# Last expert pair to its tokens through a matmul, the other expert rows loaded behind the last weights

## What is computed

```python
def hier_moe(u, w_group, b_group, w_router, b_router, w1, w3, w2):
    ...
    gate = p_grp * p_exp / jnp.sum(p_exp, axis=-1, keepdims=True)
    expert = g_sel * EXP_PER_GROUP + e_sel
    ...
    def expert_block(args):
        xe, e = args
        hid = jax.nn.silu(xe @ w1[e]) * (xe @ w3[e])
        return hid @ w2[e]

    yb = lax.map(expert_block, (xb, blk_e)).reshape(p_tot, d)
    out = jnp.zeros((n + 1, d), u.dtype).at[buf_tok].add(yb * buf_w[:, None].astype(yb.dtype))
    return out[:n]
...
    h = h + hier_moe(u, ...).reshape(b, t, d)
    return rmsnorm(h, norm_final_g)[:, N_META:]
```

## Time and profile before

| | us |
|---|---|
| median of 3 runs (2552.2 to 2559.76) | 2552.73 |
| the profiled execution, time | 2553.39 |
| its span | 2551.5 |
| PE busy / DVE busy / ACT busy / POOL busy | 2256.6 / 972.8 / 454.4 / 87.0 |

### The profile page before, as it was taken

How to read it: one execution, slowest core, us unless ns; L and a number is a source line. 1 busy time by engine, 2 the same in 40 slices (tenths; PEclk the granted TensorE clock), 3 DMA queues, 4 the chain that set the end, 5 groups by cost and what they waited for, 6 DMA issues and landing times.

```text
span 2551.5 us, 25973 instructions
## 1 busy us (share of the span) xinstructions
PE 2256.6 (88%) x9977; PEld 1536.2 (60%) x9977; DVE 972.8 (38%) x1962; ACT 454.4 (18%) x855; POOL 87.0 (3%) x118
## 2 busy tenths in 40 slices
PE   7999999988988999999899997788999688788882
PEld 5888887336753888887658774456785433223330
DVE  5454542232662554534420118866551310000003
ACT  2000000154361010001210024432013000000001
POOL 0000000000001000000110000000000000000000
PEclk9999999999999999999999998889999699988896
DMA  3232222211004232331132210000232599999994
GB/s 131 67 99 78 84 91 76 66 50 34 1 1 141 92 100 66 100 115 63 43 99 74 66 42 1 1 9 13 87 116 95 229 428 429 428 428 429 428 377 178
DMA packets 171350, 347.73 MB, mean 136 GB/s; under 512 B 17633, under 2 KB 146273, under 8 KB 154866
## 3 DMA queue, kind: packets, MB, share of 16 engines
q1 hardware_dynamic: 164960, 331.22, 35.0%
q0 software_dynamic: 5680, 12.99, 1.3%
q10 hardware_dynamic: 610, 2.17, 0.2%
HBM read 337.50 MB, written 16.98 MB: 139 GB/s over the span
## 4 chain that ended last, share of the span: by engine, by line
PE 67%; DMA 17%; DVE 7%; ACT 3%; DVEq 2%; issue 2%; SPq 0%; ACTq 0%; PEldq 0%; PEld 0%; POOLq 0%
PE PS L612 17%; DMA M<-w 11%; PE PS L643 10%; PE PS L69 7%; PE PS L3002 7%; PE PS L2367 5%; DMA M<-w_ffn_up 4%; PE PS L386 4%; PE PS L2549 2%; PE PS L924 2%; PE PS L1632 1%; PE PS L904 1%; DVE M L1958 1%; PE PS L988 1%; PE PS L1153 1%
## 5 line engine op out<-in xcount | busy, mean ns | idle before, releaser
L612 PE MATMUL PS<-M 128*128 128x256 f32 x2464 | 541.5, 382 | 16.4 <-DVE M L357 12.2
L612 PEld LDWEIGHTS PS<-M 128*128 128x128 f32 x2464 | 468.4, 191 | 90.3 <-issue 13.8
L3002 PE MATMUL PS<-M 128*64 128x512 f32 x1536 | 368.5, 639 | 86.0 <-DMA M<-w 81.6
L3002 PEld LDWEIGHTS PS<-M 128*64 128x64 f32 x1536 | 124.0, 147 | 319.0 <-issue 278.4
L643 PE MATMUL PS<-M 128*128 128x256 f32 x1232 | 268.9, 379 | 4.8 <-DVE M L731 2.5
L643 PEld LDWEIGHTS PS<-M 128*128 128x128 f32 x1232 | 233.4, 190 | 42.0 <-issue 10.8
L69 PE MATMUL PS<-M 128*128 128x264 f32 (+1 forms) x774 | 187.5, 403 | 16.5 <-DVE M L1701 5.4
L69 PEld LDWEIGHTS PS<-M 128*128 128x128 f32 x774 | 147.7, 193 | 55.4 <-issue 13.2
L3076 DVE TENSOR_TENSOR M<-M,PS 128x512 f32<-128x512 f32 x16 | 11.0, 687 | 420.9 <-PE PS L3002 420.9
L734 DVE TENSOR_TENSOR M<-M,PS 128x256 f32<-128x256 f32 x220 | 92.6, 421 | 200.8 <-PE PS L612 196.6
L2367 PE MATMUL PS<-M 128*128 128x264 f32 x616 | 142.9, 394 | 8.0 <-DVE M L2466 5.0
(11 more groups left out here) (381 smaller groups left out, 2279.0 us busy)
## 6 DMA issues: line engine op xcount, KB each, us to landing
M<-w SPq DMA_DIRECT2D x64, 2048.0 KB, 18.9
M<-w SPq DMA_DIRECT2D x64, 1024.0 KB, 21.4
M<-w_ffn_gate SPq DMA_DIRECT2D x22, 1024.0 KB, 5.4
M<-w_ffn_up SPq DMA_DIRECT2D x22, 1024.0 KB, 5.3
M<-w_ffn_down SPq DMA_DIRECT2D x16, 1024.0 KB, 5.1
M<-w_in SPq DMA_DIRECT2D x13, 1024.0 KB, 5.3
M<-w_in SPq DMA_DIRECT2D x25, 512.0 KB, 3.8
M<-w_ffn_down SPq DMA_DIRECT2D x8, 768.0 KB, 4.7
```

The costliest lines, as they stand in the source:

```text
L612: last = nc.tensor.matmul(PS[:, 3 * half + BANK[p], 0:HALF], lhs[:, a, :], rhs[:, a, :], start=p in FIRST and a == 0, stop=p in LAST and a ...
L3002: last = nc.tensor.matmul(PS[ROWS * k:ROWS * k + ROWS, bank, :], wide[:, a * P + ROWS * k:a * P + ROWS * k + ROWS], weights(k), start=star ...
```

## The change

1. `down_weights`: w2 comes in four transfers of 1 MB, in two halves of the contracted rows with a semaphore each, and `w2` has the halves outside and the banks inside. The same for all pairs.
2. `norm_final_g` is loaded at the start of the stage, ahead of w1 of the second pair, to where the gain of the earlier norm lay.
3. At the end of the routing DVE makes `C10["last"]`: for each choice of each token its gate if its pair is the last, else 0. Ahead of the last pair DVE makes ten tiles, for each of five token tiles and two choices, which have that gate in the token's slot of its row (L3123 of the kernel after), and TensorE multiplies each by the identity and sums over the choices, which gives `LAST_GATES`, slots by tokens.
4. The last pair is no more scattered. TensorE multiplies `LAST_GATES` by `YO`, two matmuls for each token tile (L3078), and DVE adds that from PSUM to `HN` (`last_pair`, L3157).
5. `rows_stored` is raised when the scatters of all other pairs have landed, and SP then loads `expert_rows` in four transfers of 1 MB and two small ones, behind the last weights in its program. Their buffers are elsewhere. The rows of the last pair in `expert_rows` are the zeros that lie there, so the weighted sum adds nothing for them.
6. The barrier behind the experts is gone, and semaphores of the routing are shared under new names.

```diff
-        C10 = {n: small(10) for n in ("rank", "pair", "half", "ob", "q", "in", "eid", "step")}
+        C10 = {n: small(10) for n in ("rank", "pair", "half", "ob", "q", "in", "eid", "step", "last")}
+        LAST_PAIR = small(1)
...
-        CG = [at(WORK0 + 18592 + 1024 * n, D) for n in range(10)]
-        GFIN = at(XN0, D)
+        CG = [at(base + 2 * D * n, 2, D) for base in (XN0, WORK0 + 8192) for n in range(2)]
+        CG4 = [at(HT0 + 3072, D), at(WORK0 + 12288, D)]
+        GFIN = GROW
+        LAST_SLOTS = [at(HT0 + 1024 + P * n, P) for n in range(8)] + [at(RG0 + 1024 + 640 + P * n, P) for n in range(2)]
+        LAST_GATES = at(RG0 + 1024, S2)
...
+            ts_(LAST_PAIR, PAIRS_F[:, 0:1], -1.0, None, ALU.add)
             then(ts_(EBI, EBF, float(EXPERTS - 1), None, ALU.min))
+            for j in range(2):
+                stt(C10["last"][:, 5 * j:5 * j + 5], C10["pair"][:, 5 * j:5 * j + 5], LAST_PAIR, C5[f"ga{j + 1}"],
+                    ALU.is_equal, ALU.mult)
+            dve.drain()
...
+            def down_weights(experts):
+                for part in range(2):
+                    for k in range(2):
+                        sp.dma_start(W2B[k][:, 2 * part:2 * part + 2, :],
+                                     expert("w2_2", experts[k], 4)[:, 2 * part:2 * part + 2, :]).then_inc(w2_in[part], 16)
...
+            sp.dma_start(GFIN, I["norm_final_g_2"].rearrange("(o n) -> o n", o=1).to_broadcast([P, D])).then_inc(gfin_in, 16)
             gate_weights(1, (1, BASE + 1))
...
-            for last in (2, 1):
-                pool.wait_ge(y_cp, pairs - last + 2)
-                scatter_rows(pool, pairs - last)
-            pool.wait_ge(y_st, pairs * 16)
+            rest = pool.value_load(PAIRS_I[0:1, 1:2], min_val=1, max_val=SPILL + 1)
+            pool.wait_ge(y_cp, rest + (BASE - 1))
+            scatter_rows(pool, rest + (BASE - 3))
+            pool.wait_ge(y_st, rest * 16 + 16 * (BASE - 2))
             pool.sem_inc(rows_stored, 1)
...
-                pe.wait_ge(w2_in, i * 32 + 32)
-                for half in range(2):
-                    for a in range(4):
+                for a in range(4):
+                    if a % 2 == 0:
+                        pe.wait_ge(w2_in[a // 2], i * 32 + 32)
+                    for half in range(2):
                         last = both(5 + half, HTT, lambda k: W2B[k][:, a, 512 * half:512 * half + 512], a,
                                     a == 0, a == 3)
...
+            pe.wait_ge(routing_given, 4)
+            for t, (lo, w) in enumerate(TOK_TILES):
+                dest = PS[:, 7, lo:lo + w] if w == P else PS[:, 4, 0:w]
+                for j in range(2):
+                    last = nc.tensor.matmul(dest, LAST_SLOTS[2 * t + j][0:w], ident[0:w, 0:w], start=j == 0, stop=j == 1)
+            last.then_inc(routing_made, 1)
             w1_w3(pe_last, 0, rest * 32 + (16 * AHEAD + 32))
+            pe.wait_ge(last_gates, 1)
             w2(pe_last)
+            pe.wait_ge(y_cp, pe_last + 2)
+            for t, (lo, w) in enumerate(TOK_TILES):
+                if t > 2:
+                    pe.wait_ge(hsum, t - 2)
+                for half in range(2):
+                    last = nc.tensor.matmul(PS[0:w, LAST_BANKS[t] + half, :], LAST_GATES[:, lo:lo + w],
+                                            YO[:, 512 * half:512 * half + 512], start=True, stop=True)
+                last.then_inc(last_added, 1)
...
+            for t, (lo, w) in enumerate(TOK_TILES):
+                for j in range(2):
+                    n = 5 * j + t
+                    ins = nc.vector.tensor_scalar(LAST_SLOTS[2 * t + j][0:w], C["iota"][0:w], C10["in"][0:w, n:n + 1],
+                                                  C10["last"][0:w, n:n + 1], ALU.is_equal, ALU.mult)
+            ins.then_inc(routing_given, 1)
+            dve.wait_ge(routing_made, 3)
+            nc.vector.tensor_copy(LAST_GATES[:, 0:S1], PS[:, 7, :])
+            nc.vector.tensor_copy(LAST_GATES[:, S1:S2], PS[:, 4, 0:META]).then_inc(last_gates, 1)
             hidden(dve_last)
             turned(dve_last)
...
+            def weighted(t):
+                w = TOK_TILES[t][1]
+                dve.wait_ge(comb_in[t], COMB_IN[t])
                 for j in range(2):
-                    ins = nc.vector.scalar_tensor_tensor(HN[0:w, t, :], CG[2 * t + j][0:w],
-                                                         C5[f"ga{j + 1}"][0:w, t:t + 1], HN[0:w, t, :], ALU.mult, ALU.add)
-                    if j:
-                        ins.then_inc(hsum, 1)
-                    else:
-                        dve.drain()
-                if t > 1:
-                    normed(t - 2)
+                    nc.vector.scalar_tensor_tensor(HN[0:w, t, :], rows_of(t, j)[0:w], C5[f"ga{j + 1}"][0:w, t:t + 1],
+                                                   HN[0:w, t, :], ALU.mult, ALU.add)
+                    dve.drain()
+
+            def last_pair(t):
+                w = TOK_TILES[t][1]
+                dve.wait_ge(last_added, t + 1)
+                row = HN[0:w, t, :].rearrange("p (c n) -> p c n", c=2)
+                nc.vector.tensor_tensor(row, row, PS[0:w, LAST_BANKS[t]:LAST_BANKS[t] + 2, :], ALU.add).then_inc(hsum, 1)
+
+            weighted(0)
+            weighted(1)
+            last_pair(0)
+            for t in range(2, 5):
+                weighted(t)
+                last_pair(t - 1)
+                normed(t - 2)
+            last_pair(4)
...
-            sp.wait_ge(stage_done, WORKERS * (PROJ2_STAGE + 6))
             sp.wait_ge(rows_stored, 1)
-            for t, (lo, w) in enumerate(TOK_TILES):
-                for j in range(2):
-                    sp.dma_start(CG[2 * t + j][0:w], y_dram[j * S2 + lo:j * S2 + lo + w, :]).then_inc(comb_in[t], 16)
-            sp.dma_start(GFIN, I["norm_final_g_2"].rearrange("(o n) -> o n", o=1).to_broadcast([P, D])).then_inc(gfin_in, 16)
+            by_choice = y_dram.rearrange("(j t) d -> t j d", j=2)
+            for t, (lo, w) in enumerate(TOK_TILES[0:4]):
+                sp.dma_start(CG[t], by_choice[lo:lo + w]).then_inc(comb_in[t], 16)
+            for j in range(2):
+                sp.dma_start(CG4[j][0:META], by_choice[S1:S2, j, :]).then_inc(comb_in[4], 16)
```

More of the change, by code:

```diff
@@ L2760, in route_act @@
         def route_act(act):
[L2761 to L2764, removed]
+            act.wait_ge(choice_in, 1)
+            nc.scalar.activation(GE, GE, ACT.Exp).then_inc(choice_out, 1)
+            act.wait_ge(choice_in, 2)
+            nc.scalar.activation(C5["ex"], C5["ex"], ACT.Exp).then_inc(choice_out, 1)
         def route_pe(pe):
-            pe.wait_ge(e_onehot, 1)
+            pe.wait_ge(routing_given, 1)
             columns = ES.rearrange("p t e -> p (t e)")
@@ L2778, in route_pe @@
                                             start=j == t == 0, stop=j == 1 and t == 4)
-            last.then_inc(buf_ready, 1)
+            last.then_inc(routing_made, 1)
         def route_dve(dve):
@@ L2818, in route_dve @@
             dve.drain()
-            tt(ES[:, 0:5, :], E12[:, 0], E12[:, 1], ALU.add).then_inc(e_onehot, 1)
+            tt(ES[:, 0:5, :], E12[:, 0], E12[:, 1], ALU.add).then_inc(routing_given, 1)
             def per_expert(name, values):
@@ L2919, in others @@
                 sp.wait_ge(y_done, i)
-                for k in range(2):
-                    sp.dma_start(W2B[k], expert("w2_2", experts[k], 4)).then_inc(w2_in, 16)
+                down_weights(experts)
             def pair(i, c):
@@ L2931, in experts_sp @@
             up_weights((0, BASE))
-            for k in range(2):
-                sp.dma_start(W2B[k], expert("w2_2", BASE * k, 4)).then_inc(w2_in, 16)
+            down_weights((0, BASE))
             sp.wait_ge(g_in, 16)
+            sp.dma_start(GFIN, I["norm_final_g_2"].rearrange("(o n) -> o n", o=1).to_broadcast([P, D])).then_inc(gfin_in, 16)
             gate_weights(1, (1, BASE + 1))
@@ L3125, in program @@
         OUT_DMAS = 5
+        COMB_IN = (16, 16, 16, 16, 32)
         def moe_sp(sp):
@@ L3139, in moe_sp @@
                 if out is not None:
-                    sp.dma_start(out[0, lo + first - META:lo + w - META, :], CG[2 * t][first:w]).then_inc(out_done, 16)
+                    rows = CG4[0] if t == 4 else CG[t][:, 0, :]
+                    sp.dma_start(out[0, lo + first - META:lo + w - META, :], rows[first:w]).then_inc(out_done, 16)
         def moe_pool(pool):
             first_rows_pool(pool); stage(pool, "pool")
-            experts_pool(pool); stage(pool, "pool")
+            experts_pool(pool)
             if dbg is not None: stage(pool, "pool")
@@ L3148, in moe_pe @@
             route_pe(pe); stage(pe, "pe")
-            experts_pe(pe); stage(pe, "pe")
+            experts_pe(pe)
             if dbg is not None: stage(pe, "pe")
@@ L3153, in moe_act @@
             route_act(act); stage(act, "act")
-            experts_act(act); stage(act, "act")
+            experts_act(act)
             final_act(act)
@@ L3159, in moe_dve @@
```

(2 more changed lines are left out.)

38 lines of the change are left out of this document (20 added, 18 removed).

## The result

The kernel after takes 2536.86 us (2532.16 to 2540.77), the kernel before beside it on the same chip 2552.73 (2550.76 to 2559.76). The ratio is 0.9927, 95% interval 0.9909 to 0.9946. The forecast was 2532.0 with 2526 to 2541: the time lies in the range, 4.9 us above the forecast and at the upper edge of its own range of 2527 to 2537; a second measurement of the same kernel (e10) got 2539.2. One run of the kernel after (3038.73 us, counted in its median alone) and one of e5 (3040.85 us), at mean granted clocks of 0.735 and 0.734, stand apart from all others and are in no range and no ratio here. The profiled execution took 2536.86, its span is 2535.0 us (before 2551.5).

The account below looks back on a forecast made before the run. The weight stream was taken to bound the expert stage, with a serial tail behind it. Terms -5.6 (last w2, start included), -18.7 (to first add), +2.7 (DVE), +0.3 (reload) took 2553.4 to 2532 us, range 2526 to 2541.

Parts of the forecast that it names:

- Bulk of the stage: nothing: Expert stage: splitting w2 into 1 MB transfers costs and gains nothing, as the stream stays at 428 GB/s.
- Start of the stage: +1.0: Stage start: extra DVE operations and the early norm_final_g shift the weight stream by 0 to 2.6 us, taken as 1.0.
- The slots-by-tokens matrix: Ahead of the last pair: DVE's ten tiles take 3.3 us, covered; TensorE's identity products add 2.5 us from 2474.1.
- w2 of pair 13 ends near 2450.3, 4.5 us earlier: Pair 13: TensorE starts w2 on its first half, ending 4.5 us earlier and filling the 2451 to 2457 us hole.
- the last w2: -5.6 us: Last pair: the last down-projection ends at 2503.0 for 2508.6, with the 1.0 us of the start included.
- The second then, since its weights are there by 2499.0 at the latest: Last w2: its second half runs directly behind the first, which ends at 2498.0, without waiting for weights.
- An idle time of 2.35 us or less did not bring it down: Last w2: idle time this short leaves the granted clock full, so 32 records take 7.3 us for 9.46.
- To the first add: From the last w2's end to DVE's first waiting add: 3.0 us in place of 21.7, a gain of 18.7.
- DVE behind it: DVE's work from that first add to its end: 21.5 us for 18.85 before, a cost of 2.7.
- Reload: +0.3: Expert-row loads: late landing of tile 0's rows delays DVE's combining by up to 1.8 us, taken as 0.3.
- (C): Rival, 10%: w2's halves don't land apart, w2 ends as before plus 1.0, clock low; +6.6 us, 2538.7.
- (B): Rival, 8%: row loads disturb the last weights' landing or start only after it; about 2541 us.

Follow-up runs that it names:

- e10: The kernel after, unchanged, measured again beside the kernel before; 2539.2 us, ratio 0.9942 to the kernel before.
- e5: The kernel before with only norm_final_g loaded early, at the start of the stage; ratio 0.9956 to the kernel before.
- e2: The kernel before with only w2 split into four half transfers and the new loop; ratio 0.9984 to the kernel before.
- e4: The kernel after with norm_final_g loaded behind the expert rows, not ahead of w1 of the second pair; ratio 0.9911 to the kernel before.
- e9: The kernel after with the edits of e4 and e7 together; ratio 0.9927 to the kernel before.
- e1: The kernel after with w2 again in two whole 2 MB transfers and the old loop; ratio 0.9943 to the kernel before.
- e3: The kernel after with the expert-row loads held until the first product of the last pair is done; ratio 0.9955 to the kernel before.
- e7: The kernel after with the expert-row loads held until w3 of the last pair is used; ratio 0.9926 to the kernel before.
- e6: The kernel after with w1 of pair 15 loaded earlier, into the second w1 buffer, row loads held until it is used; ratio 0.9942 to the kernel before.
- e8: The kernel after with the edits of e6 and e7 together; ratio 0.9944 to the kernel before.

## Why the prediction was right, and where it was not

- **Bulk of the stage: nothing. Right as far as the runs tell.** 426 GB/s for 428 over 381 us would be 1.8 us of stream. All nine executions with halves have 426 or 427, but of the three with whole w2 one (e5) has 426 too, beside 428 twice; so a small cost of the halves is neither shown nor excluded. The rule against the change fell: by the Trainium skill (DMA: Bandwidth & Descriptors, Bandwidth, Measured) 1 MB transfers would run at 341 GB/s; queued behind one another they ran at 426 here. The page's table is for loads issued from GpSimd; these are issued by SP.
- **Start of the stage: +1.0.** S is 1.2 us later, but it differs by 4.0 us between two executions of the same kernel. Of those with halves, the executions with a late gain (e2, e4, e9) end w2 at 479.2, 482.9 and 478.9, those with an early one at 478.9 to 481.6, which is not to be told from nothing. With whole w2, e5 and e1 (early gain) end it at 485.2 and 485.3 and the kernel before at 482.5, and that is about the 2.6 us of the upper bound. The term stays open. (The prediction counts four small DVE operations; the diff has three and the drain.)
- **The slots-by-tokens matrix. Right in size:** 2.59 us for the identity products (2.5), 2.63 us for DVE's ten tiles (3.3), covered; they began at 2478.04 and not at 2474.1.
- **"w2 of pair 13 ends near 2450.3, 4.5 us earlier". This step failed**, and with it "the last w2: -5.6 us". SP issues w2 of pair 14 when w2 of pair 13 is done: at 2454.33, before at 2454.82. I had taken w3's end as given and drawn w2 forward. But the stream sets the period. w2 begins as late as before (420 us behind S in both), only its wait is gone, and w3 ends 4.2 us later, 3.0 of them behind S (its successor is issued at 2444.24, before at 2440.04), held by its own landing: 5.54 us idle in the kernel after, 6.11 in e2. What w2 of pair 13 gains behind S is 1.7 us, most of it clock: behind 1.39 us of idle time, not 4.55, the 96 records from it on take 20.82 us for 22.36. Of the two holes in the stream, 0.54 x 5 for 2437 to 2442 (share 0.46, below) and 3.1 us for 2451 to 2457, one of 0.29 x 11 = 3.2 us is left. The end of the stream did not move all the same: share 0.37 from 2496 to 2499 before, 0.34 in e3, so it ends 471 to 472 us behind S in both. Why the filled hole did not bring the end forward is not shown.

The window of 2437 to 2442 us in the kernel before:

```profile
2437.00:2442.00 5.00, 4.61 (x26) 2.20 (x22) 1.56 (x2) 0.00 (x0) 0.18 (x1) 1.00 0.46 154
```

- **What was left of that term:** 2503.0 was 476.0 behind S. Measured are 481.6 in the first execution and 478.9 in e10, against 482.5 before: 0.9 and 3.6 of the 6.5 us claimed, all from the last pair, which no longer waits 4.61 us and in e10 multiplies for 7.53 us in place of 9.46. Of the 5.6 us that are missing in the first execution 4.4 are there by the end of w3 (2497.69 - 2027.25 = 470.4 for 2492.0 - 2026.0 = 466.0), and 1.2 are w2's own, at the lower clock. Of the 4.4, 2.8 are the end of w2 of pair 14, which the failed step drew forward (2478.15 - 2027.25 = 450.9 for 2474.1 - 2026.0 = 448.1), and 1.4 are a wait for w1 of pair 15, which the prediction put at nothing. That wait came in every kernel with halves and w1 in its old place (0.38 to 2.76 us) and in none with whole w2.
- **"The second then, since its weights are there by 2499.0 at the latest" was too early as well.** That is 473.0 behind S. In e3, e7, e9 and e10 TensorE waited 0.17 to 0.26 us for the second half of the last w2, and had it 475.2 to 476.1 behind S, in e3 with no row load behind it. So even there the last w2 could not end at 476.0: with 3.65 us for 16 records it ends at 478.9 at the earliest. Whole, w2 was in at 473.1, 475.4 and 475.4 (before, e5, e1) and had 9.46 to 9.90 us of work behind that landing. What the halves bring is that less work stands behind it.
- **"An idle time of 2.35 us or less did not bring it down" fell too**, in the first execution: 0.56 behind 1.41 us, 0.72 behind 0.78 us.
- **To the first add: 3.23 us for 3.0. DVE behind it: 20.57 for 21.5. Right.** The DVE term was 0.9 too high, most of it because the instruction behind an add starts 1.14 us after the add's start and not 1.31.
- **Reload: +0.3, mis-sized.** The rows of tile 0 were to land 2.6 us behind the last weights. They landed at 2505.52, 6.5 us behind the end of the stream as e3 has it (2027.25 + 471.8 = 2499.05). From there DVE needs 26.0 us in e7, e9 and e10, where it never waits for TensorE. So the rows alone set an end of 2531.5, and had the last w2 ended at 2503.0 as forecast, DVE would have ended 1.1 us earlier than it did, not 5.9. The term would have been 4.8 us then, beyond its own bound of 1.8. That is why e7, e9 and e10, with their better w2, have tails of 24.9 and not 23.8.

The sum: 482.5 + 40.6 has become 481.6 + 23.8, 17.7 us behind S, and S came 1.2 us later; the forecast had 21.3. Told by its two parts, the tail was forecast at -18.7 + 2.7 + 0.3 = -15.7 us and came at -16.8, and the end of the last w2 was forecast at -5.6 and came at +0.3 (2508.56, then 2508.86). So the time lies in the range because the tail was right and is three quarters of the gain; the w2 term gave nothing in this execution. Of the two rivals that I held likeliest each was true in part. (C): the halves do land apart (in e10 the first was in by 2502.58 and the second at 2506.46), but the clock was partly low, and the 5.6 us that the first execution lost are near its +6.6 by other steps. (B): the rows land late, not the weights.

## What to carry to other kernels

Look first at what stands last in the queue and is wanted first: one gain vector loaded earlier gave 10 us by itself, and nothing once the rows were early and the gain was asked for later (e4). Test such steps alone and together. In this loop, which the stream bounds, removing TensorE's wait for one transfer moved the wait to the next; some of the time was kept only where the loop ends, so price such a step by the last round. And the hole in the stream was no gain when it was filled with what was not wanted next (e6).

## What I had not expected of the hardware

**A transfer queued behind others lands later than its place says.** The first megabyte of rows is 2.5 us of stream, and landed 6.5 us behind the end of the weights' stream (estimated by e3's). Issue and median landing, in the kernel after (last w2, then rows), in e7 and in e3, where the rows are alone in the queue:

```profile
M<-w SPq DMA_DIRECT2D x4, 1024.0 KB, 19.2
...
M<-expert_rows SPq DMA_DIRECT2D x4, 1024.0 KB, 19.4
```

```profile
M<-expert_rows SPq DMA_DIRECT2D x4, 1024.0 KB, 12.1
```

```profile
M<-expert_rows SPq DMA_DIRECT2D x4, 1024.0 KB, 8.6
```

Issued 7.5 us later behind S in e7 (469.9 for 462.4), the first lands at nearly the same time, 478.7 for 478.3. Alone, the first takes 5.4 us (2507.89 to 2513.31). I take it that the 16 engines work through the queue at different pace, and that a landing is that of the slowest. e3 fits that: with nothing queued behind the last w2 the mean share falls to 0.34 at 2496 to 2499 us and 0.03 at 2499 to 2502, and its second half is waited for until 2500.97. No row here shows the single engines.

**The granted clock differed between executions of the same instructions.** Pair 15 began behind 0.38, 0.56, 0.77 and 0.99 us of idle time at full clock (e9, e10, e3, e7) and behind 1.39, 1.41 and 2.76 us with a drop that made 64 records take 15.65 us for 13.95 (e4, after, e2). But the last w2, behind 0.78 or 0.79 us of idle time in all of the kernels with halves, ran at full clock in e2, e3, e7, e8, e9 and e10, and took 8.78 us for 7.09 in the kernel after, in e4 and in e6. e2 had had the lower clock in pair 15's first products and had the full one here; e6 the other way round. What decides between them stays open; it was worth 1.7 us a time.
